# Experts sorted on the chip by row count: 21 blocks of 128 rows per layer in place of 24, with 4, 3 or 2 groups of 32 rows per expert

## The chip, the cores and the metric

The kernel runs on one core of one Trainium2 chip. The metric is the device time of one execution in microseconds (us), lower is better. The core has five engines that run their own instruction streams and meet at semaphores: PE (TensorE, matmuls), DVE (VectorE), ACT (ScalarE), POOL (GpSimd) and SP (SyncE, which here only issues DMAs). Sixteen DMA engines move data between the chip's large memory and the on-chip buffers.

## The reference, cut to what matters

The program is one step of a two-layer decoder with 1024 prompt tokens and 8 sample tokens, model width 1024, all in float32. Each layer ends in a mixture of experts: a router picks one of 4 groups and two of the 8 experts in it for every token, so 2 x 1032 = 2064 rows go to 32 experts.

```python
def grouped_experts(xf, expert_idx, expert_w, e_gate, e_up, e_down):
    ...
    order = jnp.argsort(flat_e)
    ...
    def run(args):
        xb, e = args
        hb = jax.nn.silu(xb @ e_gate[e]) * (xb @ e_up[e])
        return hb @ e_down[e]
    ...
    return jax.ops.segment_sum(y_rows * row_w[:, None], row_tok, num_segments=T + 1)[:T]
```

`e_gate[e]` and `e_up[e]` are 1024 x 256 and `e_down[e]` is 256 x 1024, 1 MB (1.049 million bytes) each, 3 MB per expert. Routing the inputs by the reference gives 33 to 94 rows per expert in the first layer and 44 to 94 in the second. Sorted by count, the nineteenth expert has 62 and 64 rows, and the twentieth 61 in both layers.

## The kernel before

Per layer the function `mix_route_experts` runs: output projection and layer norm of 9 token tiles (8 of 128 rows and one with the 8 samples), router logits, a gate product per tile (`gates(t)`, with the small `p_turned` and `embeddings`), and then the experts.

The router's tables are made by DVE alone, in a chain of small instructions in which each waits for the one before (`do(...)`). From the counts per expert it works out to which row of the scratch tensor XR each token's two copies go. POOL scatters the rows there (`dx_ready`), and the chain ends with `r_ready` at 2, after a table of overflow blocks has been made. PE waits for this `r_ready` after `gates(1)`, ahead of `p_turned(2)`, because two of the chain's inputs sit in PSUM banks that PE writes next:

```python
if t == 1:
    pe.wait_ge(r_ready, 2)
if t + 1 < NT:
    p_turned(t + 1)
```

In XR each expert e has a fixed place of 3 units of 32 rows (96 rows), so the 32 experts fill 96 units, or 24 blocks of 128 rows. The program calls a block a quad, q = 0 to 23. In a quad each unit of 32 rows is multiplied by the weights of its expert on a quarter of PE's columns. Per quad PE runs `gate_up(q)` (64 matmul records, line 2251), the transposes of the next block's rows (line 2149), `down(q-1)` (32 records, line 2273) and the transposes of the hidden rows (line 2260). DVE copies between them, ACT applies Silu (line 2412) and issues the store of each result block to YR (line 2408).

SP issues all loads, in one list in order of need. The weights have 5 slots (`SLOTS`): expert e uses slot e % 5, and its loads are issued when the last quad of expert e-5 is done (`gu_done` for gate and up, line 2005; `y_all_done` for down, line 2010). The row blocks have 4 slots (line 2000). Experts 0 and 1 are loaded as soon as all layer norms are done, expert 2 when 6 gate products are done, expert 3 when the last embedding product is done (its slot lies over the gate's weights), and expert 4 when the last base tile is stored.

Rows beyond an expert's 96 would go to overflow blocks, run by `rest_turns`, a loop whose number of turns is fixed when the program is built (5 in the kernel before) and whose bodies are skipped where no block is used. With counts up to 94 no overflow block is used. All engines go through the turns of this loop (lines 1835 and 1836) before the barrier that ends the phase (line 112).

Of the kernel before, what the change touches and what calls it, by code (L numbers as in the profile page):

```python
# [6 lines left out]
I32 = mybir.dt.int32  # L7
ALU = mybir.AluOpType
# [29 lines left out]
NEG = -1e30  # L38
UNIT, UNITS = 32, 3
CAP = UNIT * UNITS  # L40
QUADS = NE * CAP // P
REST = NE * CAP
BLOCKS = 2 * (SEQ + DECB) // (CAP + 1) + 1
# [1777 lines left out]
def first_quad(e):  # L1821
    return UNITS * e * UNIT // P
# [19 lines left out]
def mix_route_experts(nc, d, layer, ident, step, out):  # L1842
# [5 lines left out]
    with Phase(nc) as ph:  # L1848
# [39 lines left out]
        bincl = ph.sb("ro_bincl", [P, NE])  # L1888
        bstart = ph.sb("ro_bstart", [P, NE])
        tx = ph.sb("ro_tx", [P, NE])  # L1890
        ty = ph.sb("ro_ty", [P, NE])
# [19 lines left out]
        b1 = place.at("op_b1", R_B1, [P, D])  # L1911
        sq = place.at("op_sq", R_SQ, [P, D])
        G = place.at("ms_G", R_PT, [P, G_ALL])
        CQ = place.at("ms_CQ", R_SIG, [P, VR, DH])
# [35 lines left out]
        s_steps, s_acts, s_rep, s_ready, s_out = (ph.sem(n) for n in ("s_steps", "s_acts", "s_rep", "s_ready", "s_out"))  # L1950
        tab_loaded, dx_ready = ph.sem("tab_loaded"), ph.sem("dx_ready")
        x_in = [ph.sem(f"x_in{i}") for i in range(XSLOTS)]
        gu_in, wd_in = ([ph.sem(f"{n}{i}") for i in range(SLOTS)] for n in ("gu_in", "wd_in"))
# [10 lines left out]
        CONSTS = 16 * 7  # L1964
        assert QUADS * P == REST and QUADS >= XSLOTS and QUADS % 2 == 0
        with nc.Block() as block:
            @block.sync
            def _(sp):
# [32 lines left out]

                def load_gate_up(e, src=None, done=None):
                    s = e % SLOTS
                    for n, w in enumerate(("e_gate", "e_up")):
                        sp.dma_start(wgu[s][:, n].rearrange("p k n -> p (k n)"),
                                     d[w][layer, e].rearrange("(p k) n -> p (k n)", k=KC)).then_inc(gu_in[s], 16)

                def load_down(e):
                    s = e % SLOTS
                    sp.dma_start(wd[s][:, :].rearrange("p k n -> p (k n)"), d["e_down"][layer, e].rearrange("(p k) n -> p (k n)", k=2)).then_inc(wd_in[s], 16)  # L2010

                sp.wait_ge(h1_ready, NT)
                for e in range(2):
# [299 lines left out]
            def _(act):  # L2313
# [106 lines left out]
                for b in rest_turns(act, used):  # L2420
                    row = act.value_load(tab[0:1, ds(4 * b + 1, 1)], min_val=0, max_val=XROWS - P)
                    act.wait_ge(rest_gu, b + 1)
                    act.activation(sil[:, 0, :], gu[0][:, 0, :], ACT.Silu).then_inc(rest_sil, 1)
                    act.wait_ge(rest_out, b + 1)
                    act.dma_start(d["YR"][ds(row, P)], ye[:, 0, :]).then_inc(rest_stored, 16)

                for s in range(2):
                    act.wait_ge(base_stored[s], 16 * (NT // 2 + 1 - s))
                    act.wait_ge(stored[s], 16 * (QUADS // 2 - s))
                act.wait_ge(rest_stored, 16 * used + 16)  # L2430
# [3 lines left out]
            def _(dve):  # L2434
# [161 lines left out]
                def do(ins):  # L2596
                    q.did(ins)
                    q.wait()
# [144 lines left out]
                for s in range(2):  # L2743
                    dve.wait_ge(stored[s], 16 * (QUADS // 2 - s))
                dve.wait_ge(tab_loaded, 16)
                used = dve.value_load(tab[0:1, TOTAL:TOTAL + 1], min_val=0, max_val=BLOCKS)
                for b in rest_turns(dve, used):
# [10 lines left out]
                    for n in range(2):  # L2758
                        last = dve.tensor_copy(ye[:, 0, n * 512:(n + 1) * 512], yp[n][:, :])
                    last.then_inc(rest_out, 1)  # L2760


def combine_last(nc, d, layer, ident):
# [3 lines left out]
    with Phase(nc) as ph:  # L2767
# [20 lines left out]
        with nc.Block() as block:  # L2788
# [40 lines left out]
            @block.vector  # L2829
            def _(dve):  # L2830
                dve.memset(r1[:, TP, :], 0.0).then_inc(zeroed, 1)
                dve.memset(r2[:, TP, :], 0.0).then_inc(zeroed, 1)
# [157 lines left out]
```

## Time and profile before

| what | value |
|---|---|
| time, median of 3 runs | 2520.85 us (2516.44 to 2523.32) |
| span of the profiled execution, first to last instruction | 2513.9 us |
| what lies around the span | the three runs are 2.5 to 9.4 us above it, the median 6.9 us |
| mean granted TensorE clock over the span | 0.967 |
| PE busy | 2314.2 us, 92% of the span |
| moved by DMA | 519.82 MB, mean 207 GB/s |
| expert stage, layer 1 and layer 2 | 915 to 1208 us and 2141 to 2433 us |

The profiled execution has no time of its own beside the span. In the profile, PE is the matmul engine and PEld its weight load; a name such as `ex_wgu<-in_e_up` is what is written and what is read. A time in brackets behind an instruction is how long its engine stood idle before it and what ended that. Lines with a letter q behind the engine are of its queue or sequencer. DMA share is the mean busy share of the 16 DMA engines.

### The profile page before, as it was taken

Reading aid. Unit: us, or ns where it says so; the run is one execution under the profiler, and the core shown is the slowest. Engines: PE = TensorE matmul, PEld = TensorE weight load, DVE = VectorE, ACT = ScalarE, POOL = GpSimd, SP = SyncE. Lnnn points to the kernel's source line nnn. Section 1 sums busy time; section 2 is a strip of 40 time slices with the busy share of each in tenths; the row PEclk is TensorE's granted clock in tenths of the full one; section 3 lists DMA queues with packets and bytes.
Section 4 is the critical chain, followed back from the end, with each engine's and each line's share of the span. In section 5 each row is a group of like instructions: output and inputs, shape, how many; then the busy total and the mean of one; then the engine's idle time right before and its main releaser. Section 6 shows DMA issues by size and latency. Waiting matters only on the chain. (4 is left out here: it accounts for less than half of the span.)

```text
span 2513.9 us, 40274 instructions
## 1 busy us (share of the span) xinstructions
PE 2314.2 (92%) x15084; PEld 1189.8 (47%) x15084; DVE 1168.3 (46%) x2950; ACT 706.6 (28%) x1440; POOL 336.8 (13%) x517
## 2 busy tenths in 40 slices
PE   7999978888998999999599999688889899999977
PEld 3555545566554443333255555455755444333323
DVE  3444446655875122222345554466568631322226
ACT  2555544433311000000154555444322100000012
POOL 1011008710002000000100000395000020000011
PEclk9999989999999999999799999899899999999988
DMA  9477237632415449999653321665332352999966
GB/s 342 150 254 256 72 77 209 168 98 113 152 38 214 144 191 421 420 420 403 248 179 109 100 67 54 164 175 133 120 135 94 120 200 88 368 420 420 420 264 251
DMA packets 231710, 519.82 MB, mean 207 GB/s; under 512 B 60758, under 2 KB 138526, under 8 KB 206152
## 3 DMA queue, kind: packets, MB, share of 16 engines
q1 hardware_dynamic: 183528, 388.83, 42.4%
q0 software_dynamic: 27568, 87.20, 9.9%
q10 hardware_dynamic: 20416, 41.16, 4.4%
q8 instruction: 124, 2.03, 0.3%
q14 instruction: 74, 0.61, 0.1%
HBM read 386.05 MB, written 131.04 MB: 206 GB/s over the span
## 5 line engine op out<-in xcount | busy, mean ns | idle before, releaser
L505 PE MATMUL pj_zp<-pj_w,pj_xT 128*128 128x512 f32 (+1 forms) x1280 | 504.1, 541 | 3.1 <-DMA pj_w<-in_w_in 2.3
L2251 PE MATMUL op_bank<-ex_wgu,ex_xT 128*32 128x512 f32 x3072 | 339.5, 593 | 4.5 <-DMA ex_wgu<-in_e_up 3.1
L505 PEld LDWEIGHTS pj_zp<-pj_w,pj_xT 128*128 128x128 f32 x1280 | 225.4, 192 | 201.3 <-issue 194.2
L2100 PE MATMUL op_bank<-op_wout,op_hT 128*128 128x512 f32 x512 | 227.0, 601 | 1.5 <-DVE op_hT L2513 1.5
L2175 PE MATMUL op_bank<-op_wpg,op_hT 128*128 128x512 f32 x448 | 197.9, 600 | 0.0
L2251 PEld LDWEIGHTS op_bank<-ex_wgu,ex_xT 128*32 128x32 f32 x3072 | 97.5, 110 | 209.6 <-issue 202.8
L2273 PE MATMUL op_bank<-ex_wd,ex_hT 128*32 128x512 f32 x1536 | 174.7, 595 | 1.5 <-DVE ex_y L2730 1.5
L2734 DVE TENSOR_TENSOR ex_h<-ex_sil,op_bank 128x256 f32<-128x256 f32 x48 | 20.2, 422 | 325.5 <-ACT ex_sil L2412 325.5
L2412 ACT ACTIVATE ex_sil<-op_bank 128x256 f32<-128x256 f32 x48 | 18.4, 384 | 539.4 <-PE op_bank L2251 539.4
L2100 PEld LDWEIGHTS op_bank<-op_wout,op_hT 128*128 128x128 f32 x512 | 97.3, 193 | 119.1 <-issue 116.5
L1246 ACT ACTIVATE at_p<-at_s,at_nmx 128x640 f32<-128x640 f32 (+7 forms) x128 | 94.9, 741 | 171.3 <-DVE at_nmx L1209 170.9
L2175 PEld LDWEIGHTS op_bank<-op_wpg,op_hT 128*128 128x128 f32 x448 | 86.7, 193 | 108.9 <-issue 108.3
L1157 PE MATMUL at_tp<-ident,at_p 128*128 128x128 f32 x576 | 88.4, 280 | 34.5 <-DVE at_pT L1215 24.9
L2665 DVE TENSOR_TENSOR op_sig<-op_bank,op_sig 128x512 f32<-128x512 f32 x32 | 20.6, 686 | 189.6 <-PE op_bank L2190 189.6
L2063 POOL DMA_INDIRECT scratch_XR<-h,route_row x36 | 35.3, 979 | 507.5 <-DVEq L2705 497.1
L1147 PE MATMUL at_s<-first_qk 96*128 96x512 f32 (+3 forms) x192 | 78.3, 523 | 22.6 <-PEq L112 21.9
L1207 DVE TENSOR_REDUCE at_mx<-at_s 128x1 f32<-128x640 f32 (+7 forms) x128 | 97.0, 758 | 4.4
L476 POOL DMA_INDIRECT pj_r<-scratch_YR,route_row x18 | 19.2, 1067 | 581.3 <-issue 399.1
L1157 PEld LDWEIGHTS at_tp<-ident,at_p 128*128 128x128 f32 x576 | 62.4, 141 | 65.0 <-issue 61.1
L948 ACT ACTIVATE pj_z<-pj_zp 128x512 f32<-128x512 f32 (+1 forms) x80 | 43.2, 540 | 174.8 <-PE pj_zp L505 174.8
L2273 PEld LDWEIGHTS op_bank<-ex_wd,ex_hT 128*32 128x32 f32 x1536 | 45.6, 109 | 94.2 <-issue 87.0
L1205 DVE TENSOR_TENSOR at_s<-at_s,at_mask 128x128 f32<-128x128 f32 x128 | 38.3, 299 | 102.6 <-PE at_s L1147 100.6
(455 smaller groups left out, 3390.7 us busy)
## 6 DMA issues: line engine op xcount, KB each, us to landing
ex_wgu<-in_e_gate SPq DMA_DIRECT2D x64, 1024.0 KB, 20.9
ex_wgu<-in_e_up SPq DMA_DIRECT2D x64, 1024.0 KB, 24.2
ex_wd<-in_e_down SPq DMA_DIRECT2D x64, 1024.0 KB, 24.3
h<-scratch_XR SPq DMA_DIRECT2D x48, 512.0 KB, 25.0
scratch_YR<-ex_y ACTq DMA_DIRECT2D x48, 512.0 KB, 8.0
scratch_XR<-pj_zero POOLq DMA_DIRECT2D x41, 512.0 KB, 7.8
pj_w<-in_w_in SPq DMA_DIRECT2D x8, 2048.0 KB, 15.7
pc_ckv<-in_cache_ckv SPq DMA_DIRECT2D x200, 64.0 KB, 2.0
```

The lines of the kernel that those rows point to most:

```text
L505: last = pe.matmul(zp[c % ZB][:, 0:cn], xT[:, t % 2, k, :], w[:, k, c0:c0 + cn], start=(k == 0), stop=(k == KC - 1), skip_group_check=True)
L948: act.activation(z[:, t % 2, c0:c0 + cn], zp[c % ZB][:, 0:cn], ACT.Copy).then_inc(z_ready, 1)
L1147: last = pe.matmul(scores_of(n)[:, c:min(c + 512, width)], queries(j, s)[:, qb * P:(qb + 1) * P], keys(j, s)[:, c:min(c + 512, width)], st ...
L1157: last = pe.transpose(tp[e][:, kb % 4, :], probs[small(n)][units[n][1]][:, kb, :], ident[:, :])
L1205: st.did(dve.tensor_tensor(diag, diag, mask[:, :], ALU.add))
L1207: st.did(dve.tensor_reduce(mx[:, k:k + 1], out[:, 0:(qb + 1) * P], AX.X, ALU.max))
L1246: act.activation(probs[small(n)][s][:, 0:qb + 1, :].rearrange("p b n -> p (b n)"), scores_of(n)[:, 0:(qb + 1) * P], ACT.Exp, bias=nmx[:, k ...
L2063: pool.indirect_dma_start(d["XR"], bass.IndirectOffsetOnAxis(ap=dx[0:m, k, t:t + 1], axis=0), h1[0:m, t, :], None, bounds_check=XROWS - P ...
L2100: last = pe.matmul(op[n][:, :], hT[:, t, c, :], wout[:, c, n * 512:(n + 1) * 512], start=(c == 0), stop=(c == KC - 1))
L2175: last = pe.matmul(gpair[t % 2][n][:, :], hT[:, t, c, :], wpg[:, c, n * 512:(n + 1) * 512], start=(c == 0), stop=(c == KC - 1))
L2251: last = pe.matmul(gu[q % 2][part], xT[:, q % 2, c, part], wgu[s][:, :, c, :], start=(c == 0), stop=(c == KC - 1), skip_group_check=True)
L2273: last = pe.matmul(yp[n][part, :], heT[:, q % 2, c, part], wd[s][:, c, n * 512:(n + 1) * 512], start=(c == 0), stop=(c == 1), skip_group_c ...
```

## The change

The experts are ranked on the chip by their row count, ties by number. The place in that order decides the room: the first expert gets 4 units of 32 rows (128 rows), the next 18 get 3 units, the last 13 get 2 units (64 rows). That is 4 + 54 + 26 = 84 units, 21 quads. The turns of the experts in time are: the largest, then 13 pairs of one with 2 units and one with 3, then the remaining 5 with 3 units (`TURNS`). Since the program no longer knows which expert has which turn, DVE writes the expert numbers in order of turn to a table (`turnp`), a small DMA copies it into one partition (`turn`), and SP reads a number from it into a register ahead of each weight load. The size of the overflow loop follows from the smallest room: `BLOCKS` goes from 22 to 32, and `rest_turns` from 5 turns to 7. With the counts above again no overflow block is used.

```diff
-UNIT, UNITS = 32, 3
-CAP = UNIT * UNITS
+UNIT, CAP = 32, 64
+TRIPLES = 19
+TWOS = NE - TRIPLES
+TURNS = [4] + [n for _ in range(TWOS) for n in (2, 3)] + [3] * (TRIPLES - TWOS - 1)
+QUADS = sum(TURNS) * UNIT // P
...
 def last_quad(e):
-    return (UNITS * (e + 1) - 1) * UNIT // P
+    return (sum(TURNS[:e + 1]) - 1) * UNIT // P
 def experts_of(q):
-    return [(4 * q + j) // UNITS for j in range(4)]
+    units = [e for e in range(NE) for _ in range(TURNS[e])]
+    return units[4 * q:4 * q + 4]
...
-                def load_gate_up(e, src=None, done=None):
+                def load_gate_up(e):
                     s = e % SLOTS
+                    expert = sp.value_load(turn[0:1, e:e + 1], min_val=0, max_val=NE - 1)
                     for n, w in enumerate(("e_gate", "e_up")):
...
-                                     d[w][layer, e].rearrange("(p k) n -> p (k n)", k=KC)).then_inc(gu_in[s], 16)
+                                     d[w][ds(layer, 1), ds(expert, 1)].rearrange("l e (p k) n -> (l e p) (k n)", k=KC)).then_inc(gu_in[s], 16)
...
-                sp.wait_ge(h1_ready, NT)
+                sp.wait_ge(turn_ready, 1)
+                sp.dma_start(turn[:, :].rearrange("o (b n) -> o b n", n=1), turnp[0:NE, :]).then_inc(turn_loaded, 16)
+                sp.wait_ge(turn_loaded, 16)
                 for e in range(2):
                     load_gate_up(e)
                     load_down(e)
...
                 used = sp.value_load(tab[0:1, TOTAL:TOTAL + 1], min_val=0, max_val=BLOCKS)
+                sp.wait_ge(y_all_done, QUADS)
                 for b in rest_turns(sp, used):
...
-                do(TS(cnt[:, :], cnt[:, :], float(CAP), 0.0, ALU.subtract, ALU.max))
+                do(dve.scalar_tensor_tensor(key[:, :], cnt[:, :], float(2 * NE), idx[:, :], ALU.mult, ALU.subtract))
+                do(TT(among[:, :, :], key[:, :].unsqueeze(1).broadcast_to([P, NE, NE]), key[:, :].unsqueeze(2).broadcast_to([P, NE, NE]), ALU.is_gt))
+                do(dve.tensor_reduce(order[:, :], among[:, :, :], AX.X, ALU.add))
...
+                do(dve.tensor_reduce(turnf[:, :], key[:, :], AX.X, ALU.add))
+                do(dve.tensor_copy(turnp[:, :], turnf[:, :]))
+                dve.sem_inc(turn_ready, 1)
...
-                do(TS(tx[:, :], idx[:, :], float(CAP), None, ALU.mult))
-                do(dve.scalar_tensor_tensor(ty[:, :], start[:, :], float(REST - CAP), tx[:, :], ALU.add, ALU.subtract))
-                do(TS(big[:, :, :], rank[:, :, :], float(CAP), None, ALU.is_ge))
+                do(dve.scalar_tensor_tensor(ty[:, :], start[:, :], float(REST), tx[:, :], ALU.add, ALU.subtract))
+                do(TT(ty[:, :], ty[:, :], cap[:, :], ALU.subtract))
+                do(TT(big[:, :, :], rank[:, :, :], cap[:, :].unsqueeze(1).broadcast_to([P, NT, NE]), ALU.is_ge))
```

The load of the down weights is changed like that of gate and up. In the last phase DVE's two memsets of gather buffers now wait until the last rows are stored, which the gathers behind them waited for already. With 21 quads the overflow blocks use the other half of the result buffer, and the waits for stored blocks count 20 in place of 23.

The next two pieces show DVE's instructions of the first layer behind the sums over tiles (`ro_cnt` are the counts per expert, `ro_rank` each token's place in its expert, `ro_key`, `ro_among`, `ro_order` the new ranking). Before:

```order
L2683 TENSOR_TENSOR ro_cnt<-op_bank,ro_pre 128x32
L2684 TENSOR_TENSOR ro_rank<-op_bank,ro_pre 128x288
L2686 TENSOR_SCALAR ro_cnt<-ro_cnt 128x32
L2687 TENSOR_SCALAR ro_cnti<-ro_cnt 128x32
L2688 TENSOR_SCALAR ro_cnti<-ro_cnti 128x32
L2689 CAST ro_nb<-ro_cnti 128x32
```

With the change, the first 12 rows of the same place:

```order
L2702 TENSOR_TENSOR ro_cnt<-op_bank,ro_pre 128x32
L2703 TENSOR_TENSOR ro_rank<-op_bank,ro_pre 128x288
L2705 SCALAR_TENSOR_TENSOR ro_key<-ro_cnt,ro_idx 128x32
L2706 TENSOR_TENSOR ro_among<-ro_key 128x1024
L2707 TENSOR_REDUCE ro_order<-ro_among 128x32
L2709 TENSOR_SCALAR ro_tx<-ro_order 128x32
L2710 TENSOR_SCALAR ro_ty<-ro_order 128x32
L2711 TENSOR_TENSOR ro_key<-ro_tx,ro_ty 128x32
L2712 TENSOR_SCALAR ro_cap<-ro_key 128x32
L2713 TENSOR_SCALAR ro_late<-ro_order 128x32
L2714 TENSOR_SCALAR ro_key<-ro_late 128x32
L2715 TENSOR_TENSOR ro_key<-ro_key,ro_tx 128x32
```

Between `ro_rank` and the first `ro_cnti` there are now 23 instructions in place of 1; two of the 23 work on 1024 elements a partition. Further down, one instruction is added and one removed (the multiply by the fixed room goes, a subtract comes), and the comparison of 288 elements reads the table of rooms. The write of `ro_turnp` is the sixteenth of the 23.

The next two pieces are SP's queue of the first layer, from its last load of the layer norm's input to the first expert. Before:

```order
L1970 DMA h<-out_y_all 128x1024
L2005 DMA ex_wgu_9166<-in_e_gate 128x2048
L2005 DMA ex_wgu_9166<-in_e_up 128x2048
L2010 DMA ex_wd_9171<-in_e_down 128x2048
L2005 DMA ex_wgu_9167<-in_e_gate 128x2048
L2005 DMA ex_wgu_9167<-in_e_up 128x2048
L2010 DMA ex_wd_9172<-in_e_down 128x2048
L2017 DMA ex_tab<-ro_tab 1x128x4
```

With the change (`ex_turn` is the table of turns, ISA are register instructions):

```order
L1983 DMA h<-out_y_all 128x1024
L2029 DMA ex_turn<-ro_turnp 1x32x1
L2017 TENSOR_LOAD ex_turn
L2017 ISA x2
L2019 ISA
L2019 DMA ex_wgu_9163<-in_e_gate 128x2048
L2019 DMA ex_wgu_9163<-in_e_up 128x2048
L2024 TENSOR_LOAD ex_turn
L2024 ISA x2
L2025 ISA
L2025 DMA ex_wd_9168<-in_e_down 128x2048
```

The loads themselves have the same size and the same place in the list. In front of the first stands the copy of the table of turns, and each pair of gate and up loads, and each down load, has a register load and three register instructions ahead of it.

## Rows read from the trace of the kernel before

**Rows 1.** The page: busy time by engine, and DMA busy tenths in 40 slices.

```profile
PE 2314.2 (92%) x15084; PEld 1189.8 (47%) x15084; DVE 1168.3 (46%) x2950; ACT 706.6 (28%) x1440; POOL 336.8 (13%) x517
...
DMA  9477237632415449999653321665332352999966
```

**Rows 2.** Timeline of PE, expert stage: start, duration in us, instructions, idle before.

```profile
936.29 7.07 PE L2251 MATMUL op_bank<-ex_wgu,ex_xT 128*32 128x512 f32 x64
...
948.39 7.07 PE L2251 MATMUL op_bank<-ex_wgu,ex_xT 128*32 128x512 f32 x64
...
1180.15 7.07 PE L2251 MATMUL op_bank<-ex_wgu,ex_xT 128*32 128x512 f32 x64 [1.01 <-DMA ex_wgu<-in_e_up]
...
1192.25 7.07 PE L2251 MATMUL op_bank<-ex_wgu,ex_xT 128*32 128x512 f32 x64
...
1203.95 3.64 PE L2273 MATMUL op_bank<-ex_wd,ex_hT 128*32 128x512 f32 x32 [0.76 <-DVE ex_y L2730]
```

**Rows 3.** Waits of 940 to 1230 us: total us, times, longest.

```profile
PE op_bank L2251 <- DMA ex_wgu<-in_e_up: 1.6, 2, 1.0
```

**Rows 4.** Windows: busy per engine, granted clock, DMA share, GB/s (last three).

```profile
930.00:1190.00 260.00, 258.36 (x2265) 91.03 (x2260) 71.60 (x129) 8.45 (x22) 0.00 (x0) 1.00 1.01 419
2160.00:2415.00 255.00, 253.51 (x2223) 89.08 (x2219) 69.91 (x126) 8.06 (x21) 0.00 (x0) 1.00 1.01 419
...
1190.00:1195.00 5.00, 5.00 (x50) 1.62 (x46) 1.71 (x3) 0.00 (x0) 0.00 (x0) 1.00 0.52 215
```

**Rows 5.** DMA issues of 915 to 1210 us: count, size, us to landing.

```profile
ex_wgu<-in_e_up SPq DMA_DIRECT2D x29, 1024.0 KB, 25.6
```

**Rows 6.** Timeline of SP's queue, expert stage.

```profile
915.23 0.33 SPq L2005 DMA_DIRECT2D ex_wgu<-in_e_gate  x1
...
1165.99 13.10 SPq L2010 DMA_DIRECT2D ex_wd<-in_e_down  x2
```

**Rows 7.** Timeline of PE around the routing, first layer.

```profile
784.03 1.30 PE L2235 MATMUL op_bank<-ro_OS,ro_ones 128*128 128x288 f32 x2 [4.61 <-ACT op_pT L2379]
...
786.08 15.71 PE L2175 MATMUL op_bank<-op_wpg,op_hT 128*128 128x512 f32 x32
801.62 0.39 PE L2139 MATMUL op_bank<-ident,op_p 128*128 128x128 f32 x2
...
805.28 13.90 PE L2175 MATMUL op_bank<-op_wpg,op_hT 128*128 128x512 f32 x32
```

**Rows 8.** DVE's routing chain (timeline), and two groups of wide instructions.

```profile
790.25 0.18 DVE L2687 TENSOR_SCALAR ro_cnti<-ro_cnt 128x32 int32<-128x32 f32 x1
790.46 0.18 DVE L2688 TENSOR_SCALAR ro_cnti<-ro_cnti 128x32 int32<-128x32 int32 x1
...
798.77 0.17 DVE L2717 CAST ro_tab<-ro_tabf 128x4 int32<-128x4 f32 x1
...
L2507 DVE TENSOR_TENSOR op_y<-op_y,op_ss 128x1024 f32<-128x1024 f32 x16 | 19.6, 1225 | 0.5
...
L2501 DVE TENSOR_REDUCE op_ss<-op_sq 128x16 f32<-128x1024 f32 x16 | 19.4, 1215 | 13.1 <-ACT op_sq L2335 13.1
```

**Rows 9.** Windows around two idle stretches of PE (columns as in Rows 4).

```profile
780.00:784.00 4.00, 0.00 (x0) 0.01 (x1) 3.65 (x18) 2.86 (x5) 0.00 (x0) 0.86 0.40 149
784.00:786.00 2.00, 1.97 (x4) 1.51 (x5) 1.86 (x6) 0.00 (x0) 0.00 (x0) 0.50 0.00 0
...
1207.00:1213.00 6.00, 0.59 (x8) 0.00 (x0) 0.69 (x1) 0.00 (x0) 0.00 (x0) 1.00 0.24 94
1213.00:1216.00 3.00, 0.00 (x0) 0.00 (x0) 0.00 (x0) 0.09 (x1) 0.00 (x0) 0.50 0.00 0
```

**Rows 10.** The overflow loop's turns on PE's sequencer, end of the first layer.

```profile
L1835 PEldq ALU_OP  x5: 36/36/45, 1210.2 to 1213.3; - x5
```

**Rows 11.** SP's queue ahead of the expert stage, first layer.

```profile
764.22 0.33 SPq L2005 DMA_DIRECT2D ex_wgu<-in_e_gate  x1
...
825.74 17.56 SPq L2000 DMA_DIRECT2D h<-scratch_XR  x4
```

More of the change, by code:

```diff
@@ L38 @@
 NEG = -1e30
-UNIT, UNITS = 32, 3
-CAP = UNIT * UNITS
-QUADS = NE * CAP // P
-REST = NE * CAP
+UNIT, CAP = 32, 64
[3 more added lines that the diff above has]
+QUADS = sum(TURNS) * UNIT // P
+REST = sum(TURNS) * UNIT
 BLOCKS = 2 * (SEQ + DECB) // (CAP + 1) + 1
@@ L1821, in first_quad @@
 def first_quad(e):
-    return UNITS * e * UNIT // P
+    return sum(TURNS[:e]) * UNIT // P
 def last_quad(e):
-    return (UNITS * (e + 1) - 1) * UNIT // P
+    return (sum(TURNS[:e + 1]) - 1) * UNIT // P
 def experts_of(q):
-    return [(4 * q + j) // UNITS for j in range(4)]
+    units = [e for e in range(NE) for _ in range(TURNS[e])]
+    return units[4 * q:4 * q + 4]
 def rest_turns(eng, used):
@@ L1889, in mix_route_experts @@
         bstart = ph.sb("ro_bstart", [P, NE])
+        key = ph.sb("ro_key", [P, NE])
+        cap = ph.sb("ro_cap", [P, NE])
+        late = ph.sb("ro_late", [P, NE])
+        order = ph.sb("ro_order", [P, NE])
+        turnf = ph.sb("ro_turnf", [P, 1])
+        turnp = ph.sb("ro_turnp", [P, 1], I32)
+        turn = ph.sb("ex_turn", [1, NE], I32)
         tx = ph.sb("ro_tx", [P, NE])
@@ L1912, in mix_route_experts @@
         sq = place.at("op_sq", R_SQ, [P, D])
+        among = place.at("ro_among", R_SQ, [P, NE, NE])
         G = place.at("ms_G", R_PT, [P, G_ALL])
@@ L1964, in mix_route_experts @@
         CONSTS = 16 * 7
-        assert QUADS * P == REST and QUADS >= XSLOTS and QUADS % 2 == 0
+        assert len(TURNS) == NE and QUADS * P == REST and QUADS >= XSLOTS
+        RS = QUADS % 2
         with nc.Block() as block:
@@ L2000, in load_rows @@
                     sp.dma_start(xe[:, q % XSLOTS, :], d["XR"][rows(q)]).then_inc(x_in[q % XSLOTS], 16)
[L2002 removed]
+                def load_gate_up(e):
                     s = e % SLOTS
+                    expert = sp.value_load(turn[0:1, e:e + 1], min_val=0, max_val=NE - 1)
                     for n, w in enumerate(("e_gate", "e_up")):
                         sp.dma_start(wgu[s][:, n].rearrange("p k n -> p (k n)"),
[L2006 removed]
+                                     d[w][ds(layer, 1), ds(expert, 1)].rearrange("l e (p k) n -> (l e p) (k n)", k=KC)).then_inc(gu_in[s], 16)
                 def load_down(e):
                     s = e % SLOTS
[L2010 to L2012 removed]
+                    expert = sp.value_load(turn[0:1, e:e + 1], min_val=0, max_val=NE - 1)
+                    sp.dma_start(wd[s][:, :].rearrange("p k n -> p (k n)"),
+                                 d["e_down"][ds(layer, 1), ds(expert, 1)].rearrange("l e (p k) n -> (l e p) (k n)", k=2)).then_inc(wd_in[s], 16)
+                sp.wait_ge(turn_ready, 1)
+                sp.dma_start(turn[:, :].rearrange("o (b n) -> o b n", n=1), turnp[0:NE, :]).then_inc(turn_loaded, 16)
+                sp.wait_ge(turn_loaded, 16)
                 for e in range(2):
@@ L2424, in _ @@
                     act.wait_ge(rest_out, b + 1)
-                    act.dma_start(d["YR"][ds(row, P)], ye[:, 0, :]).then_inc(rest_stored, 16)
+                    act.dma_start(d["YR"][ds(row, P)], ye[:, RS, :]).then_inc(rest_stored, 16)
                 for s in range(2):
                     act.wait_ge(base_stored[s], 16 * (NT // 2 + 1 - s))
-                    act.wait_ge(stored[s], 16 * (QUADS // 2 - s))
+                    act.wait_ge(stored[s], 16 * len(range(s, QUADS - 1, 2)))
                 act.wait_ge(rest_stored, 16 * used + 16)
@@ L2743, in _ @@
                 for s in range(2):
-                    dve.wait_ge(stored[s], 16 * (QUADS // 2 - s))
+                    dve.wait_ge(stored[s], 16 * len(range(s, QUADS - 1, 2)))
                 dve.wait_ge(tab_loaded, 16)
@@ L2758, in _ @@
                     for n in range(2):
-                        last = dve.tensor_copy(ye[:, 0, n * 512:(n + 1) * 512], yp[n][:, :])
+                        last = dve.tensor_copy(ye[:, RS, n * 512:(n + 1) * 512], yp[n][:, :])
                     last.then_inc(rest_out, 1)
@@ L2830, in _ @@
             def _(dve):
+                dve.wait_ge(d["sw"]["last_rows"], 16 * LAYERS)
                 dve.memset(r1[:, TP, :], 0.0).then_inc(zeroed, 1)
```

19 lines of the change are left out of this document (added).

## The prediction, on record before the changed kernel ran

> **What bounds the kernel now.** I read the page first. PE is busy for 92% of the span and no other engine for more than half [rows 1], so as a whole the kernel looks bound by PE, and 3 blocks fewer of PE work in each layer look like a gain. But the DMA digits on the same page are 9 in a run of slices before the middle and in another near the end, and those are the two expert stages. So I read that stage by itself, in the timeline of PE, in the waits and in windows. A quad starts every 12.10 us (936.29 to 948.39) and PE has no gap in it [rows 2]. In the same stretch the DMA engines are busy for 1.01 of the time and move 419 GB/s, in both layers [rows 4]. Both are at their limit at once. Which of them ends last? Near the end two quads start late, for the gate and up weights: 1.6 us in all, with a longest wait of 1.0 us [rows 2, 3]. A weight load lands 25.6 us after its issue though its size needs 2.5 us at 419 GB/s [rows 4, 5], and two late issues take SP's queue 13.10 us where one took 0.33 [rows 6]: so much is under way that no more is taken. The stage begins with the weights of three experts in place and more asked for, DMA falls behind a little in each quad, and by quad 21 the lead is used up. DMA has its last work done at about 1192.6 us (share 0.52 of the window from 1190) [rows 4], just when quad 23's gate_up starts at 1192.25, and from there it is 15.3 us to the end of its down product at 1207.59 [rows 2].
>
> **The stage, as PE sees it.** 21 quads in place of 24 take away 3 x 12.10 = 36.3 us per layer.
>
> **The stage, as DMA sees it.** The weights stay whole: experts 3 to 31, loaded from 915.23 us on [rows 6], are 29 x 3 x 1.049 = 91.2 MB. Each row block is half a load's size. Before, 20 blocks are loaded and some 22 stored while weights still come, 22.0 MB; with the change 17 and 19, 18.9 MB. So 113.2 MB become 110.1 MB, and at 419 GB/s 270.2 us become 262.8 us: 7.5 us per layer, not 36.3. PE would need 254 us for its 21 quads, less than DMA's 263, so DMA ends last. The other 28.8 us return as waits of PE for `ex_wgu` and `ex_wd`. They come early, because a pair of experts with 2 and 3 units asks for two experts' weights in 5 units: five quads now need 8 experts, 25.2 MB, and 5.2 MB of rows in and out, 30.4 MB or 72.6 us of DMA against 60.5 us of PE. I take -7.5 us; half a per cent of the rate is 1.3 us either way.
>
> The Trainium skill speaks against this reading (DMA: Bandwidth & Descriptors, Specifications): it puts the fabric's ceiling at 435 GB/s. By that, 110.1 MB would take 253 us, under PE's 254, and the stage would be PE's and shorter by most of the 36.3 us. The trace does not agree: both stages hold 419 [rows 4].
>
> **DVE's longer chain.** PE ends `gates(1)` at 801.62 and goes on at once [rows 7]; DVE's table, whose `r_ready` it waits for, is done at 798.94 [rows 8]. So there are 2.7 us of slack. The change puts 21 small instructions, one every 0.21 us (790.25 to 790.46), I take 0.22 for the two-operand ones among them, and two wide ones of 1.23 and 1.22 us into the chain [rows 8]: 4.6 + 2.5 us. One small one goes, and one of 288 elements reads a second operand, for 0.15 us at most: 7.1 us in all. PE then waits 7.1 - 2.7 = 4.4 us, and I write 4.5 with the semaphore. Behind that wait in PE's queue stand `p_turned(2)`, all remaining gate products and the experts; PE has no gap from there to the expert stage, and the load of expert 3 waits for the last of them, so the DMA-bound stage starts as much later. This is paid in full: +4.5 us per layer, 4.2 to 4.8.
>
> **The clock after that wait.** Idle for 4.61 us in the same layer, PE was granted half its clock, 1.2 of 2.4 GHz, at its end and behind it (0.86 in 780 to 784, 0.50 in 784 to 786), and the gate product after it took 15.71 us where the next took 13.90; with the small products before it that is 1.8 + 1.1 = 2.9 us lost (for the 1.1: 2.05 us for four records of 288 columns that at 13.90/32 us per 512 columns are about 1) [rows 7, 9]. But from 1207 to 1213, idle for over 5 us after steady work, the clock stood at 1.00 still [rows 9]. The new wait follows steady work too. The price is 0 to 2.9 us; I take half, +1.5.
>
> **SP's loads.** Experts 0 and 1 are loaded from 764.22 before, and now after the table of turns, some 35 us later; they are needed at 915. The row loads come once the scatter is done, at 825.74 before [rows 11], about 7 us later now and sharing the DMA engines with two experts' weights (6.3 MB, 15 us), so near 848; the first is used at 910. The register loads and register instructions ahead of each load come ahead of loads that wait in line anyway in the stage [rows 6]. All this costs nothing; if that cover were gone, a late first load would cost what it lands after 915. Expert 4, issued at 927, is now needed by quad 2 in place of quad 3; a wait for it is part of the 28.8 us.
>
> **The overflow loop** is passed without work, but each turn takes PE's sequencer (1213.3 - 1210.2) / 4 = 0.78 us at the end of a layer [rows 10], and PE is the last to the barrier. Two turns more: +1.5 us per layer (1.2 to 1.8, as DVE and SP have turns of their own). SP's new wait for the last quad ends when PE's work ends, and hides behind that.
>
> **The clock in the stage.** A wait for weights can halve the clock as well, at up to 2.9 us. In the stretch of pairs this hides: 60.5 us of PE work plus three such losses is 69.2, under 72.6. Behind the last wait before the final experts with 3 units nothing makes it good: 0 to 2.9, I take +1.
>
> **The sum.** -7.5 + 4.5 + 1.5 + 1.5 + 1.0 = +1.0 us per layer, +2 us in all. The profiled execution's span of 2513.9 becomes 2515.9, and the median of the runs, which stands 6.9 us above that span, 2520.85 + 2 = 2523 us. The likeliest case's own range: low -7.5 - 1.3 + 4.2 + 0 + 1.2 + 0 = -3.4, high -7.5 + 1.3 + 4.8 + 2.9 + 1.8 + 2.9 = +6.2 per layer, so 2514 to 2533. A measurement of this kernel can tell about 0.3% (7.6 us) from no change, that is 2513.3 to 2528.4.
>
> **The rivals.**
> *PE bounds the stage* (0.07). If DMA could give more than 433 GB/s (a quad's 5.24 MB in 12.10 us), the whole 36.3 us come: -36.3 + 4.5 + 1.5 + 1.5 = -28.8 per layer, 2463 us. For it: PE is at 92% and waits for DMA only 1.6 us. Against it: share 1.01, the issues held up, and the same 419 twice [rows 3, 4, 6].
> *The front wait costs nothing* (0.10): the added instructions are faster than their like, or PE's wait hides. Then -7.5 + 1.5 = -6 to -5 with the tail's clock, 2510 us. Against it: the slack is 2.7 us, and the two wide instructions alone take 2.5.
> *The clock decides, and the kernel is slower* (0.10). 28.8 us of waits in pieces like the 4.61 us one are about 6 per layer. If each halves the clock and none of it hides, 6 x 2.9 = 17.4 us per layer come on top of the +1.5 at the front, in place of the tail's 1: +17.4 per layer, 2556 us. It decides once five quads hold more than four such losses, as 60.5 + 4 x 2.9 = 72.1 us reaches DMA's 72.6. Against it: PE's slow work is done while DMA fills slots, and the waits get shorter by as much. The Trainium skill has this case (TensorE: Matmul & The Clock Gate, HAM oscillation): a kernel whose waits for DMA recur between bursts of products pays for the low clock every time. Here the trace shows the drop after 4.61 us, and no run has yet shown it in this stage.
> The likeliest case has the rest, 0.73.
>
> **From the cases to numbers.** Faster by over 0.3%: 0.07 + most of the 0.10 at 2510 + a little of the likeliest = 0.17. Slower: 0.10 + 0.08 from the upper end of the likeliest = 0.18. Within: 0.65. The range leaves out both far rivals (0.17) and takes in 2510: 2509 to 2534 us.
>
> **What the changed profile would show.** The expert stages take about 285 us from the first gate_up to the last down product in place of 293, with 21 gate_ups, DMA share 1.01 and 419 GB/s; PE waits some 29 us per layer for `ex_wgu` and `ex_wd`, in the first 15 quads, and the granted clock dips there. PE stands idle 4 to 5 us at `p_turned(2)` in both layers, so the first gate_up starts near 919.5 to 922.5. Waits near zero in the stage, or a rate over 425, would prove me wrong on the limit; an expert stage over 290 us would mean that the clock or the order of loads makes DMA idle.

## The result, and the profile after

The changed kernel takes 2527.11 us (median of 14 runs, 2518.9 to 2531.22). The kernel before, on the same chip, takes 2520.64 us (14 runs, 2516.44 to 2524.58). The ratio is 1.0025, 95% interval 1.0017 to 1.0033: 6 us more, inside the 0.3% that the prediction counts as no change. Measured again later, the ratio was 1.0022 [1.0013, 1.0031]. The profile shown here is of the shortest of the 14 executions (2518.9 us); the second profile of the same kernel, further down, is of one of 2527.09 us.

The page of the changed kernel's profile, with its span, the busy times, the DMA digits and two groups of the experts (count, busy us, mean ns, then idle time ahead and what ended it), answers to [rows 1]:

```profile
span 2517.2 us, 39745 instructions
...
PE 2263.1 (90%) x14448; PEld 1172.7 (47%) x14448; DVE 1160.5 (46%) x2958; ACT 703.9 (28%) x1434; POOL 335.4 (13%) x514
...
DMA  9476127632412549999653321665332072899966
...
L2270 PE MATMUL op_bank<-ex_wgu,ex_xT 128*32 128x512 f32 x2688 | 310.0, 615 | 31.2 <-DMA ex_wgu<-in_e_up 29.7
...
L2292 PE MATMUL op_bank<-ex_wd,ex_hT 128*32 128x512 f32 x1344 | 158.4, 613 | 16.2 <-DMA ex_wd<-in_e_down 14.7
```

PE has 51 us less work in the whole program, and waits 44.4 us for expert weights. The DMA digits show the same two runs of nines, a slice shorter in the second. The mean granted clock fell from 0.967 to 0.958.

PE's timeline of the first layer, around the routing and in the expert stage, answers to [rows 7] and [rows 2]:

```profile
787.33 1.30 PE L2254 MATMUL op_bank<-ro_OS,ro_ones 128*128 128x288 f32 x2 [4.61 <-ACT op_pT L2398]
...
809.58 0.70 PE L2158 MATMUL op_bank<-ident,op_p 128*128 128x128 f32 x2 [4.95 <-DVEq L2761]
810.08 4.84 PE L2209 MATMUL op_bank<-op_wpe,op_pT 128*128 128x512 f32 x8
814.76 13.90 PE L2194 MATMUL op_bank<-op_wpg,op_hT 128*128 128x512 f32 x32
...
924.46 7.05 PE L2270 MATMUL op_bank<-ex_wgu,ex_xT 128*32 128x512 f32 x64
...
973.83 8.33 PE L2270 MATMUL op_bank<-ex_wgu,ex_xT 128*32 128x512 f32 x64 [3.65 <-DMA ex_wgu<-in_e_up]
...
1019.10 9.59 PE L2270 MATMUL op_bank<-ex_wgu,ex_xT 128*32 128x512 f32 x64 [5.38 <-DMA ex_wgu<-in_e_up]
...
1069.69 6.45 PE L2292 MATMUL op_bank<-ex_wd,ex_hT 128*32 128x512 f32 x32 [3.33 <-DMA ex_wd<-in_e_down]
...
1195.78 7.07 PE L2270 MATMUL op_bank<-ex_wgu,ex_xT 128*32 128x512 f32 x64
...
1207.47 3.64 PE L2292 MATMUL op_bank<-ex_wd,ex_hT 128*32 128x512 f32 x32 [0.76 <-DVE ex_y L2773]
```

Read it in two pieces. From the first product of the routing (`ro_ones`) to the first gate_up it is 137.14 us, and was 784.03 to 914.99 = 130.96; in the second layer 137.43 for 130.71. I call this piece the front. From there to the end of the last down product, the expert stage, it is 286.65 and 286.52 us for 292.60 and 292.40. The routing itself starts 3.3 us later in this profile; that is no part of the change, for it starts between 786.2 and 789.4 us in every other profile of the study, those of the kernel before with an edit behind this place among them.

The new waits for weights, 920 to 1215 us (total us, times, longest), answer to [rows 3]:

```profile
PE op_bank L2270 <- DMA ex_wgu<-in_e_up: 14.3, 5, 5.4
...
PE op_bank L2292 <- DMA ex_wd<-in_e_down: 7.2, 3, 3.3
```

And windows of both stages, of the stage's tail, of the products behind the front's wait, and behind three waits in the stage (last three columns: granted clock, DMA share, GB/s), answer to [rows 4] and [rows 9]:

```profile
940.00:1195.00 255.00, 233.41 (x1956) 81.93 (x1948) 62.30 (x112) 7.29 (x19) 0.00 (x0) 0.95 1.01 418
2170.00:2410.00 240.00, 217.11 (x1824) 76.28 (x1820) 57.66 (x104) 6.52 (x17) 0.00 (x0) 0.96 1.01 419
1190.00:1195.00 5.00, 5.00 (x48) 1.91 (x40) 2.31 (x4) 0.38 (x1) 0.00 (x0) 1.00 0.83 343
...
810.00:815.00 5.00, 5.00 (x11) 2.22 (x10) 0.04 (x1) 0.38 (x1) 3.78 (x5) 0.74 1.00 380
...
974.00:977.00 3.00, 3.00 (x20) 0.80 (x19) 0.00 (x0) 0.00 (x0) 0.00 (x0) 0.60 0.98 410
...
1020.00:1026.00 6.00, 6.00 (x44) 1.67 (x40) 0.00 (x0) 0.00 (x0) 0.00 (x0) 0.65 1.00 418
1070.00:1076.00 6.00, 6.00 (x32) 1.35 (x24) 0.69 (x1) 0.00 (x0) 0.00 (x0) 0.55 1.03 426
```

So DMA is as full as before, at the same rate, while PE has idled and run near half clock in pieces. The simple reading, that 3 quads of 12.10 us fewer make each stage 36.3 us shorter, fails: it is 6 us shorter.

### The profile page after: what moved, and what is told of

Read it like the earlier page. It is cut to its first block and busy times, and to the rows that moved or that the text cites. A ratio compares the mean times of both kernels' runs of the same rounds, so it can differ in the third digit from the quotient of the medians.

```text
span 2517.2 us, 39745 instructions
## 1 busy us (share of the span) xinstructions
PE 2263.1 (90%) x14448; PEld 1172.7 (47%) x14448; DVE 1160.5 (46%) x2958; ACT 703.9 (28%) x1434; POOL 335.4 (13%) x514
## 5 line engine op out<-in xcount | busy, mean ns | idle before, releaser
L2270 PE MATMUL op_bank<-ex_wgu,ex_xT 128*32 128x512 f32 x2688 | 310.0, 615 | 31.2 <-DMA ex_wgu<-in_e_up 29.7
L2270 PEld LDWEIGHTS op_bank<-ex_wgu,ex_xT 128*32 128x32 f32 x2688 | 89.9, 113 | 219.6 <-issue 214.3
L2292 PE MATMUL op_bank<-ex_wd,ex_hT 128*32 128x512 f32 x1344 | 158.4, 613 | 16.2 <-DMA ex_wd<-in_e_down 14.7
```

The source lines that it names most:

```text
L2270: last = pe.matmul(gu[q % 2][part], xT[:, q % 2, c, part], wgu[s][:, :, c, :], start=(c == 0), stop=(c == KC - 1), skip_group_check=True)
L2292: last = pe.matmul(yp[n][part, :], heT[:, q % 2, c, part], wd[s][:, c, n * 512:(n + 1) * 512], start=(c == 0), stop=(c == 1), skip_group_c ...
```

## The experiments

The theory on trial was the prediction's balance: DMA bounds the stage, the longer DVE chain is paid in full ahead of it, the turns of the overflow loop cost a little, and SP's additions nothing. All ratios are against the kernel before, on the same chip.

### The wait for DVE, taken away by a shorter one

PE waits for the routing chain because two of its inputs sit in PSUM. The last read of them is `ro_rank`, near the start of the chain. Here PE waits for a semaphore raised right behind that read, so none of the added instructions is ahead of it. The same edit was made in the kernel before (`b_free`), where PE never waited.

```diff
                     if t == 1:
-                        pe.wait_ge(r_ready, 2)
+                        pe.wait_ge(r_read, 1)
...
                 bef[:, 0:NT * NE], pre[:, :, :].rearrange("p t e -> p (t e)"), ALU.add))
+                dve.sem_inc(r_read, 1)
```

Expected of the changed kernel with it, and of the kernel before with it:

> The changed kernel, in which PE waits after gates(1) only until DVE has read the two PSUM banks (right behind the sums ro_cnt and ro_rank), and not until its whole table is done. Theory (the chain's end holds PE up, once per layer, with a clock drop behind it): the idle 4.95 us and the slow products behind it go, 6.2 and 6.7 us less to the first gate_up in the two layers, so about 12.5 us faster than the changed kernel, 2514 us, and faster than the kernel before by about 6 us. Rival (the front wait only starts the DMA-bound stage later and the stage would be as long from wherever its loads can start, or the loss comes back elsewhere): within 3 us of the changed kernel.

> The kernel before with the same shorter wait. Theory: there the chain's end had 2.7 us of slack, so nothing changes: within 2 us of the kernel before. Rival (the shorter wait helps by itself, whatever the chain's length): several us faster, and then the gain in the changed kernel would not measure what its longer chain costs.

The changed kernel takes 2511.12 us with it, ratio 0.9966 [0.9954, 0.9977]; the kernel before 2519.72 us, ratio 0.9999 [0.9990, 1.0008]. The timeline of PE in the changed kernel with the short wait:

```profile
788.86 15.45 PE L2194 MATMUL op_bank<-op_wpg,op_hT 128*128 128x512 f32 x32
804.15 0.39 PE L2158 MATMUL op_bank<-ident,op_p 128*128 128x128 f32 x2
804.38 3.60 PE L2209 MATMUL op_bank<-op_wpe,op_pT 128*128 128x512 f32 x8
```

No idle time stands in brackets, and the small products have their old durations (0.39 and 3.60 for 0.70 and 4.84). The fronts are 130.71 and 130.81 us, as before the change. The wait and its clock cost 6.4 and 6.6 us per layer by the fronts, and the times agree (some 15 us between the ratios 1.0025 and 0.9966, with intervals of about 2 and 3 us either way). Without it, the change is a gain of 8.6 us (2519.72 to 2511.12, both kernels with the short wait).

### The added chain alone, in the kernel before

The other way round: two wide and 21 small DVE instructions on tiles of their own, put where the change puts its ranking, and nothing else changed.

```diff
+                do(TT(among[:, :, :], cnt[:, :].unsqueeze(1).broadcast_to([P, NE, NE]), cnt[:, :].unsqueeze(2).broadcast_to([P, NE, NE]), ALU.is_gt))
+                do(dve.tensor_reduce(pad[:, :], among[:, :, :], AX.X, ALU.add))
+                for _ in range(11):
+                    do(TS(pad[:, :], pad[:, :], 1.0, None, ALU.mult))
+                for _ in range(10):
+                    do(TT(pad[:, :], pad[:, :], cnt[:, :], ALU.max))
                 do(TS(cnt[:, :], cnt[:, :], float(CAP), 0.0, ALU.subtract, ALU.max))
```

> The kernel before with DVE's chain made longer by as much as in the changed kernel, and nothing else of the change: two wide instructions (1024 elements) and 21 small ones between the sums and the table. Theory (the front costs 6.2 to 6.7 us per layer by itself, clock drop included, and is paid in full): 12 to 14 us slower than the kernel before, 2533 us. Rival (the shorter wait's gain of some 15 us in the changed kernel came from something else than the chain): less than 9 us slower.

It takes 2535.86 us, ratio 1.0069 [1.0055, 1.0082]: 14 to 21 us more. PE's timeline in it:

```profile
809.20 0.55 PE L2141 MATMUL op_bank<-ident,op_p 128*128 128x128 f32 x2 [4.55 <-DVEq L2726]
809.54 5.29 PE L2192 MATMUL op_bank<-op_wpe,op_pT 128*128 128x512 f32 x8
```

The fronts are 137.38 and 138.26 us, the stages 292.60 and 292.83 as before. The fronts make 14.0 us of it, at the lower end of the interval; 1.8 us more lie between the first stage and the second routing (804.1 us for 802.3), where the edit changes nothing. So the chain alone does what the front of the changed kernel does, and the stage behind it isn't touched.

### Whose is the stage: less to load

In both kernels, from the sixth expert in time on, the up weights are loaded for one partition of 128; the other 127 keep an earlier expert's weights. That is 1 of 3 MB less per expert, and no work of PE less.

```diff
+                        m = 1 if n == 1 and e >= SLOTS else P
-                        sp.dma_start(wgu[s][:, n].rearrange("p k n -> p (k n)"),
-                                     d[w][layer, e].rearrange("(p k) n -> p (k n)", k=KC)).then_inc(gu_in[s], 16)
+                        sp.dma_start(wgu[s][0:m, n].rearrange("p k n -> p (k n)"),
+                                     d[w][layer, e].rearrange("(p k) n -> p (k n)", k=KC)[0:m]).then_inc(gu_in[s], 16)
```

> The kernel before, which from the sixth expert on loads only 1 of the 128 partitions of the up weights (the rest stays that of an earlier expert, so 27 of 32 experts compute with wrong up weights): 28 MB less per layer, a third of the weights. PE's work is the same. Theory (PE and DMA are both at their limit before, DMA by a hair): the 1.6 us of waits per layer go, the quads keep their 12.10 us: 2517 us, 0 to 5 us faster than the kernel before. Rival (DMA alone sets the stage, or its traffic slows PE): much more than 5 us faster.

> The changed kernel with the same lighter loads of the up weights (1 of 128 partitions from the sixth expert on, the rest wrong). Theory (DMA holds the changed stage up): 21 quads at 12.10 us with no waits and no clock drops, so the stage goes from 286.7 to about 257 us, the 36.3 us per layer of the 3 removed quads come in full, and the whole is about 2467 us, some 60 us under the changed kernel and 50 under the light kernel before. Rival (what PE waits for is the order or the lateness of the issues, not the bytes): the stage stays above 275 us, over 2500 us in all.

The kernel before with light loads takes 2514.0 us, ratio 0.9978 [0.9969, 0.9987]; the changed one 2455.27 us, ratio 0.9742 [0.9727, 0.9757]. The window of the stage in the changed kernel with light loads (busy PE second, then at the end clock, DMA share, GB/s):

```profile
930.00:1170.00 240.00, 239.31 (x2104) 83.29 (x2100) 65.29 (x118) 8.22 (x21) 0.00 (x0) 1.00 0.89 341
```

And that of the kernel before with light loads:

```profile
930.00:1190.00 260.00, 260.00 (x2286) 89.96 (x2282) 69.97 (x126) 8.06 (x21) 0.00 (x0) 1.00 0.88 317
```

Here PE has hardly a gap and its full clock, and DMA has room. The stage is 290.75 us before and 254.44 us with the change, and in the second layer the same to 0.01 us: 36.3 less, the 3 quads of 12.10. This is the prediction's rival "PE bounds the stage", made true by taking load off DMA. The kernel before gains only 1.7 to 1.9 us per stage from the light loads, and the changed one 32: before, DMA and PE ended nearly together, and with the change DMA alone sets the pace.

### The small suspects: loop turns, SP's registers

The overflow loop with 5 turns in place of 7, all else as changed:

```diff
-    with eng.Fori(0, -(-BLOCKS // SLOTS)) as r:
+    with eng.Fori(0, 5) as r:
```

> The changed kernel with 5 turns of the overflow loop in place of 7 (no overflow block is used with these inputs, so nothing else changes). Theory of the prediction (0.78 us a turn on PE, the last to the barrier): 3 us faster than the changed kernel. Rival (another engine or a fixed cost ends last at the barrier, as the two profiles hint with +0.0 and +1.3 us): 0 to 1.3 us faster.

It takes 2524.22 us, ratio 1.0017 [1.0008, 1.0026], against 1.0025 and 1.0022 for 7 turns: 1 to 2 us less, within the intervals. The trace is finer. From the last down product to PE's next work are 25.64 us in the first layer and 13.09 in the second with 5 turns, and 27.07 and 14.33 with 7. The kernel before has 27.15 and 13.06. So two turns cost 1.3 to 1.4 us, but in the first layer that is not seen in the comparison, because PE's first pass of the branch got shorter. The branch in the kernel before (count, shortest, median and longest ns, first and last start):

```profile
L1836 PEldq COMPARE_BRANCH  x5: 221/221/3891, 1206.3 to 1213.1; - x5
L1836 DVEq COMPARE_BRANCH  x5: 62/63/77, 1208.8 to 1212.0; - x5
```

and in the changed kernel:

```profile
L1839 PEldq COMPARE_BRANCH  x7: 221/221/2411, 1209.8 to 1216.6; - x7
...
L1839 DVEq COMPARE_BRANCH  x7: 63/63/77, 1212.3 to 1217.0; - x7
```

PE's longest is 3.89 us before and 2.41 after, and DVE's last branch now starts later than PE's. The long first pass takes 3.65 to 3.89 us in the four profiles of the kernel before and its variants, and 2.41 to 3.31 us in the nine of changed kernels; why was not tried.

Then the weight loads at fixed addresses, without the copy of the table of turns, the wait for it and SP's register loads; the rows then meet the weights of other experts.

```diff
-                    expert = sp.value_load(turn[0:1, e:e + 1], min_val=0, max_val=NE - 1)
...
-                                     d[w][ds(layer, 1), ds(expert, 1)].rearrange("l e (p k) n -> (l e p) (k n)", k=KC)).then_inc(gu_in[s], 16)
+                                     d[w][layer, e].rearrange("(p k) n -> p (k n)", k=KC)).then_inc(gu_in[s], 16)
```

> The changed kernel with the weight loads at fixed addresses in the order of expert numbers, no table of turns copied and no register loads on SP, and the first two experts loaded once the layer norms are done, as before. It leaves out that the rows meet their own expert's weights (a block gets those of another expert). Theory (SP's additions are hidden): within 2 us of the changed kernel. Rival (register loads ahead of the DMAs or the later first loads cost time): faster by the 4 us that the changed kernel is above the sum of the parts seen in its profile.

2525.74 us, ratio 1.0021 [1.0012, 1.0030]: no difference to 1.0022 that can be told. Fronts 137.26 and 137.51, stages 285.62 and 287.74. SP's additions and the 35 us later first loads are hidden, as forecast.

### The order of the turns

The stage is DMA's, but is its tail, the part behind the last loads? In the changed kernel's timeline the last wait for a weight ends at 1143.37 us, and from there to the end PE waits for no load. Two more orders of the same rooms: all threes first and the twos last, and the reverse. The tables of places that DVE works out follow.

```diff
-TURNS = [4] + [n for _ in range(TWOS) for n in (2, 3)] + [3] * (TRIPLES - TWOS - 1)
+TURNS = [4] + [3] * (TRIPLES - 1) + [2] * TWOS
```

```diff
-TURNS = [4] + [n for _ in range(TWOS) for n in (2, 3)] + [3] * (TRIPLES - TWOS - 1)
+TURNS = [4] + [2] * TWOS + [3] * (TRIPLES - 1)
```

> The changed kernel with another order of turns: the largest, then all 18 experts with 3 units, then the 13 with 2 units; as many DVE instructions, the same bytes, the same blocks. Theory (the bytes alone set when DMA ends, and the stage's end follows it): DMA is busy to the same time, PE's waits of some 20 us move to the last 6 blocks, and since the last load now meets PE waiting for it, the end comes up to 5 us per layer earlier: 2517 to 2527 us. Rival (alternating twos and threes is what keeps DMA busy; twos in a row drain the slots): longer than the changed kernel by the waits that DMA's idle time then adds, over 2535 us.

> The changed kernel with the third order of turns: the largest, then the 13 experts with 2 units, then the 18 with 3; same bytes, blocks and number of DVE instructions. Theory (DMA's end is set by the bytes, and the stage's end by what is left to do after the last weights): PE waits early, then runs the threes at DMA's pace, so the last weights are used a block or more after they land, as in the changed kernel: within 4 us of it, and 8 to 16 us slower than with the threes first. Rival (long stretches of one size are what helps, at either end): as fast as with the threes first, 2513 us.

Threes first: 2512.97 us, ratio 0.9977 [0.9968, 0.9986]. Twos first: 2525.36 us, ratio 1.0027 [1.0017, 1.0036], as changed. The stages are 281.14 and 281.10 us with threes first, and 287.58 and 287.44 with twos first. PE's timeline of the last quads, threes first:

```profile
1126.92 9.37 PE L2270 MATMUL op_bank<-ex_wgu,ex_xT 128*32 128x512 f32 x64 [10.26 <-DMA ex_wgu<-in_e_up]
...
1158.25 9.07 PE L2270 MATMUL op_bank<-ex_wgu,ex_xT 128*32 128x512 f32 x64 [4.76 <-DMA ex_wgu<-in_e_up]
...
1174.21 7.07 PE L2270 MATMUL op_bank<-ex_wgu,ex_xT 128*32 128x512 f32 x64 [1.80 <-DMA ex_wgu<-in_e_up]
...
1190.35 8.38 PE L2270 MATMUL op_bank<-ex_wgu,ex_xT 128*32 128x512 f32 x64 [3.38 <-DMA ex_wgu<-in_e_up]
...
1203.35 3.64 PE L2292 MATMUL op_bank<-ex_wd,ex_hT 128*32 128x512 f32 x32 [0.75 <-DVE ex_y L2773]
```

and a window near its end:

```profile
1190.00:1195.00 5.00, 4.65 (x32) 1.44 (x36) 0.00 (x0) 0.00 (x0) 0.00 (x0) 0.70 1.02 420
```

DMA moves the same bytes (112.57 MB around the stage, 112.55 as changed) and its share falls below 1 at about the same distance from the stage's start: at 1195 us here, 269 us behind it (0.71 in the next 1 us), and at 1192 as changed, 268 us behind it (0.86 in the next 1 us). What differs is PE's work behind it. SP's queue issues the last gate and up weights when an earlier expert frees their slot, and that comes equally early, 242.9 us into the stage as changed and 242.2 with threes first:

```profile
1167.33 0.33 SPq L2019 DMA_DIRECT2D ex_wgu<-in_e_gate  x1
```

```profile
1168.09 0.33 SPq L2019 DMA_DIRECT2D ex_wgu<-in_e_gate  x1
```

The first row is of the changed kernel, the second of threes first. From this issue to the end of the stage the changed kernel takes 1211.12 - 1167.33 = 43.79 us. Twos first takes the same 43.79 (1170.31 to 1214.10), though it is a kernel with another history. The five experts whose weights lie in the slots then have 3 units each, PE works on them without waiting for a load, and the last load lands before PE wants it: this tail is PE's. It is not new: in the kernel before, whose last experts have 3 units too, the last issue comes 246.3 us into the stage and 46.3 us follow, with the 1.6 us of waits in them. With twos last there is less to compute on the same five slots. PE stands waiting when the load lands, 22.3 us after the issue, and 16.6 us of work follow (8.38 of them a slow gate_up), 38.9 us together. Counted from the stage's start the last gate_up comes 6.8 us earlier and the rest takes 1.3 us longer, which is the 5.5 us between 286.65 and 281.14.

### Both gains together

> Both edits together: PE's shorter wait for the two PSUM banks, and all experts with 3 units ahead of those with 2. Theory (the two act in different places, and add): 8.7 us under the kernel before from the first, and 0 to 10 us more from the second, 2502 to 2512 us. Rival (both feed the same DMA-bound stage and the second adds nothing): 2511 us, as with the first alone.

The short wait and threes first: 2498.67 us (5 runs, 2495.18 to 2505.14), ratio 0.9919 [0.9906, 0.9933]. The fronts are 130.99 and 130.80 us, the stages 283.07 and 280.20. The two gains add up, and this kernel is faster than both that the study began with: 20 us under the kernel before.

### The changed kernel again

> The changed kernel once more, unchanged, beside the two above. The parts seen in one pair of profiles (front +12.9, stages -11.8, end of layers +1.2 us) sum to +2.3 us over the kernel before, the first measurement said +6.5. If that was the measurement's own error, the ratio comes nearer 1.001; if a part of the change acts that the two profiles do not show, it stays at 1.0025 or above.

2524.77 us, ratio 1.0022 [1.0013, 1.0031]. Fronts 137.46 twice, stages 288.11 and 287.82. So the stage varies between profiles by over a microsecond, where the front does not. PE's timeline shows where. The last wait for a weight, in the shown profile and then in the second one:

```profile
1143.37 3.64 PE L2292 MATMUL op_bank<-ex_wd,ex_hT 128*32 128x512 f32 x32 [1.69 <-DMA ex_wd<-in_e_down]
```

```profile
1144.64 5.34 PE L2292 MATMUL op_bank<-ex_wd,ex_hT 128*32 128x512 f32 x32 [3.60 <-DMA ex_wd<-in_e_down]
```

Behind this wait the down product ran at full clock in one and 1.70 us slower in the other (granted clock 0.72 in 1144 to 1150). The eight stages of the four profiles with this order and all loads by the table:

| kernel, layer | slow work ahead of the last wait, us | last wait ends, us into the stage | slow work behind it, us | stage, us |
|---|---|---|---|---|
| changed, 1 | 10.0 | 218.9 | 0 | 286.65 |
| changed, 2 | 8.6 | 218.8 | 0 | 286.52 |
| changed again, 1 | 8.8 | 218.7 | 1.70 | 288.11 |
| changed again, 2 | 8.8 | 218.4 | 1.70 | 287.82 |
| short wait, 1 | 9.4 | 219.3 | 1.63 | 288.67 |
| short wait, 2 | 10.1 | 218.5 | 1.70 | 287.89 |
| 5 turns, 1 | 11.6 | 219.3 | 0 | 287.05 |
| 5 turns, 2 | 8.3 | 218.9 | 1.70 | 288.39 |

Slow work is the time of gate_up and down products beyond 7.07 and 3.64 us. From the last wait's end PE needs 67.7 us in every row, plus the slow work behind it. Ahead of it, 3.3 us more or less of slow work move the wait's end by under 1 us. So a clock drop is hidden as long as another wait for DMA follows, and paid in full behind the last. The mean of the eight stages is 287.6 us.

## Why the prediction was right, point by point

The forecast was 2523 us, most likely within 0.3% of no change; measured were 2527.11 and 2524.77 us. The likeliest case is the one that took place. Its terms, per layer:

- **The stage is DMA's, -7.5.** The limit is shown: share 1.01 at 418 and 419 GB/s, as in [rows 4], and PE gets its whole 36.3 us only when load is taken off DMA. The size was 1.6 us too large: without the slow work behind the last wait the eight stages take 286.1 to 287.1 us, 5.9 us less than before on the mean. The bytes fell by 3.0 MB (115.53 MB around the stage before, 112.55 after), forecast 3.1, and from 45 to 265 us into the stage both kernels move 92.4 MB. But in the first 45 us DMA is less full than before. The windows of the kernel before and of the changed one:

```profile
914.99:959.99 45.00, 44.31 (x394) 15.52 (x386) 14.51 (x26) 2.82 (x5) 0.00 (x0) 1.00 0.97 380
```

```profile
924.46:969.46 45.00, 44.23 (x394) 15.93 (x386) 14.50 (x26) 2.82 (x5) 0.00 (x0) 1.00 0.91 365
```

  That is 0.7 MB less, or 1.6 us at 420 GB/s, at a start that the forecast took as equal. No run tried to fill it. The Trainium skill's ceiling (DMA: Bandwidth & Descriptors, Specifications), 435 GB/s, was not reached in a stage of any kernel.
- **A clock loss in the tail, +1.0.** It comes in five of the eight stages, at 1.63 to 1.70 us, and not in the other three: 1.05 us on the mean. The mechanism is the one forecast; that the size fits is luck, for +1.0 was picked from 0 to 2.9. The net of both terms was forecast at -6.5; it is -5.9 in the shown profile, which had no such loss, and -4.5 in the second, which had it. That PE has 43.79 us of work behind the last issue, of which another order gives back 5.5, the forecast didn't ask.
- **The waits, "some 29 us" per layer.** 21.5 us, in 8 waits. The rest of the 36.3 us less came back as slow work: gate_ups of 8.33, 9.59 and twice 8.77 us for 7.07 and a down product of 6.45 for 3.64, 9.99 us in all. -36.3 + (21.5 - 1.6) + 10.0 = -6.4, near the stage's -5.95. The first ends at 973.83 us, in the fifth quad, and the last at 1143.37 us, at the down product of the fifteenth; the forecast was the first 15 quads.
- **DVE's chain, +4.5, and the clock behind it, +1.5.** Shown twice, by taking the wait away and by making it alone. The wait is 4.95 us and the chain ends 7.2 us later against the routing's start (forecast 7.1). The embedding products take 4.84 us for 3.60 and the small ones 0.70 for 0.39: 1.55 us for the clock. Sum 6.2 to 6.7 against 6.0. It was written that the granted clock might stay up, and it fell, to 0.74 in 810 to 815 us; the drop cost about half of its upper bound. Half was taken for want of anything better, so this fit is luck too. The first gate_up comes at 924.46 us, past the forecast's 919.5 to 922.5, because the routing starts 3.3 us later in this profile.
- **The turns, +1.5.** 1.27 us in the second layer, -0.1 in the first, where PE's long first pass of the branch shortened. Right in size where the same first pass is compared (5 turns against 7: 1.43 and 1.24).
- **SP's loads at nothing.** Shown by the fixed addresses. The row loads start at 843.88 us, for the forecast "near 848".

The sum by measured terms, both layers: in the shown profile fronts +12.9, stages -11.8, turns +1.2, so +2.3 us; in the second profile of the same kernel +13.3, -9.1 and +1.3, so +5.5 us. The times say +6.3 (4.3 to 8.3) and +5.5 (3.3 to 7.8). The first profile is of an execution 8.2 us under its median, and what its sum lacks lies within what executions differ by: from the end of the first stage to the second routing, which the change touches only with its turns, the profiles have 800.6 to 806.6 us.

Of the rivals, "the front wait costs nothing" was false as it stood, but its price holds: forecast 2510 us, and with the wait taken away 2511.12. "PE bounds the stage" was false, and its price was right too: 28.8 us per layer less were forecast, and with light loads the change is worth 2514.0 - 2455.27 = 58.7 us, 29.4 per layer. "The clock decides" was false: it put the kernel at 2556 us. The clock does fall behind the waits in the stage, to 0.60, 0.65 and 0.55 in the windows above, with five slow groups of products in the first layer, as the Trainium skill describes for recurring waits (TensorE: Matmul & The Clock Gate, HAM oscillation). That the low clock is paid every time, as that section has it, these stages do not show: DMA's share stays at 0.98 to 1.03 through the drops, and the last wait ends at 218.4 to 219.3 us whether 8.3 or 11.6 us were lost ahead of it. A kernel with the waits and without any drop was not run. One reading of the prediction was coarse without harm: DMA's end at 1192.6 us is a mean over a window of 5 us; in shorter windows the share is 0.82 from 1188 on and still 0.81 in the last of the five.

## What to carry to other kernels

Where two engines are both full in a stage, removing work of one buys only the difference: read the DMA share of the stage, and price the change by bytes before counting matmuls. Work that is added to a chain of small dependent instructions costs from the point where its slack is used up; if someone waits for that chain only because of a buffer, let him wait for the last read of the buffer. A drop of the clock behind a wait for DMA costs nothing here while more such waits follow; count only the one behind the last. Where transfers set the pace, put last the work that needs the most bytes per product, so that little is left to compute when the last byte lands.

## What the runs showed of the hardware that was not expected

The price of a wait in clock doesn't follow its length alone. The wait of 4.95 us in the changed kernel cost 1.55 us behind it, and one of 4.55 us in the kernel before with the chain added cost 1.85 (5.29 for 3.60 and 0.55 for 0.39). In the stage, gate_ups behind waits of 1.78 and of 3.29 us both took 8.77 us, and the down product behind the last wait took 5.34 us after a wait of 3.60 (changed again) and 3.64 after one of 3.41 (fixed addresses, first layer). The first pass of a skipped loop's branch on PE took 2.4 to 3.9 us, as much as three to five later turns of 0.78 us. And DMA held 413 to 420 GB/s over 240 to 260 us in every kernel with whole weights, whatever the order of the loads.
